# Compression with token pairs stationary over four column groups; queries, scores and top-k in four parts of two heads

## The chip, the cores and the metric

The kernel runs on one core of one Trainium2 chip, in float32 throughout. The metric is the device time of one execution in microseconds (us), the median over the runs shown. TensorE (PE) multiplies matrices, VectorE (DVE), ScalarE (ACT) and GpSimd (POOL) do the elementwise work, SyncE (SP) issues the plain loads and stores, and 16 DMA engines move the data.

## The reference, cut to what matters

One decoder layer on a prompt of 512 tokens and on 8 decoding sequences of 4 tokens (32 rows). After an attention and convolution half comes PEER: every token picks 16 experts for each of 8 heads and adds their rows.

```python
# compress: 16-token chunks; a block's hidden row is the sum over its two chunks
parts = jnp.einsum('bcsgd,jsdh->jbcgh', r, w1c)          # w1: 2048 x 256 for keys and for values
hid = b1 + pe.reshape(-1) @ w1
for j in range(ratio): hid = hid + parts[j, :, j:j + nc]
out = jax.nn.gelu(hid) @ w2 + b2
# peer: D_MODEL 1024, 8 heads, 128 keys a half, 16384 experts
q = (xb @ q_w).reshape(PEER_BLOCK, PEER_HEADS, 2, PEER_DQ // 2)
s = jnp.einsum('thcd,hcnd->thcn', q, sub_keys)
s1, i1 = lax.top_k(s[:, :, 0], PEER_TOPK); s2, i2 = lax.top_k(s[:, :, 1], PEER_TOPK)
cand = s1[..., :, None] + s2[..., None, :]               # 256 candidates, of which top_k takes 16
u = eu[eidx]; v = ev[eidx]                               # rows of 1024 floats each
a = jax.nn.gelu(jnp.einsum('td,thkd->thk', xb, u))
return jnp.einsum('thk,thkd->td', g * a, v)
```

## The kernel before, in words

The tokens are worked on in five tiles: four of 128 prompt rows (0 to 3) and tile 4 with the 32 sample rows. For a tile of 128 rows, PEER needs 128 "rows" of the stream: row n is one head and one rank, and one indirect DMA of POOL (L1950) gathers for it the expert's u and v for all 128 tokens, 1 MB. Tile 4 packs four heads on the partitions and needs 32. So 544 gathers flow through a ring of 10 buffers (`RING`, tile `expert_rows`). For each row DVE makes the dot product with h2 (L1906), ACT makes the gelu, the weight and a diagonal (L1386, L1392, L1402), and PE multiplies diagonal by v into four banks (L1044, L1047 for tile 4). POOL issues the gather of row n when PE has freed row n - 10.

Everything else of a tile (norm, input products, compression, attention, convolution, output product, queries, scores and top-k) is **side work**, written as stages that are cut into slots (generators that `yield`). Tile 0's side work runs ahead of the stream (the first window), and that of tiles 1 to 4 inside it: `slots_before` spreads the slots over the rows in proportion to lengths given in `SLOTS_OF` (in rows), so that the last slot comes at row 500. Before row n each engine runs all slots that `e.before` gives, in the order of the plan (`make_plan`); a list of lists in the plan holds lanes whose slots go in step. PE runs four rows ahead (`LEAD`). PE, ACT and DVE each have one fixed order, so whatever waits in a slot holds back the rows behind it.

The side weights come in units of 1 MB through 3 slots (`SLOTS`, tile `weight_units`), issued by SP in the order of use; the load of unit j waits until unit j - 3 was used. Side work uses four banks in turn (`Products`).

The stages of the change. **cmp(i)** (PE L728, 16 slots of PE's own): 4 units of w1 (keys and values, 2 each), for each 8 positions and 2 halves of the hidden width a product with the 128x128 weights stationary and 14 to 21 chunk columns moving; then gelu (ACT L1188), w2 (PE L745) and the key norm. It is 22 slots and 11 rows long, in a lane with att(i); conv(i), the 124 taps of DVE (L1518), three in a slot, is the other lane. For tile 0 the convolution is POOL's and the other lane is a gap of 22 slots and ada2, which takes 12 units of w_ada (L608). **query0(i)** turns h2 (L882), makes the first 8 query columns from 4 units of peer_q (L848) and their scores with a unit of keys of 512 KB (L870); **query1(i)** does the second half. **topk0(i), topk1(i)** (DVE L1707 to L1758) pick the experts of four heads each; topk0 stands in a lane beside query1, topk1 beside the x and glu stages of the next tile. POOL waits for topk0 before a tile's first row and for topk1 before its row 64.

## Time and profile before

| | us |
|---|---|
| median of 3 runs | 2129.03 |
| lowest, highest | 2128.95, 2151.08 |
| span of the profiled execution, first to last instruction | 2124.2 |

The profiled execution's own time is not listed apart from its span; the lowest run and the median are 4.8 us above that span. In the span PE is busy 1587.9 us (75%), DVE 1232.5 (58%), ACT 781.4 (37%) and POOL 701.2 (33%). The DMA engines move 782.11 MB, of which the gathers' queue has 570.46, at a mean of 368 GB/s. In a table of windows, the DMA column is the busy share of the 16 DMA engines and the last one what they moved.

### The profile page before, as it was taken

What the parts mean: (1) busy time and instruction counts of PE and PEld (TensorE: products, weight loads), DVE (VectorE), ACT (ScalarE), POOL (GpSimd) and SP (SyncE); (2) the same over time, 40 slices, a digit from 0 to 9 for tenths busy, and PEclk for the clock granted to TensorE, in tenths of its full rate; (3) what the DMA queues carried; (4) which work ended last, traced back from release to release, by engine and by line L of the source; (5) the groups of instructions that cost most, each with busy time, mean ns of one, the idle gap of its engine ahead of it and who ended that gap; (6) DMA issues with size and microseconds to landing.
All of it is one profiled execution on the core that took longest, in us unless ns stands there. A gap on an engine that the chain in (4) does not pass through costs nothing.

```text
span 2124.2 us, 29781 instructions
## 1 busy us (share of the span) xinstructions
PE 1587.9 (75%) x10176; PEld 954.1 (45%) x10176; DVE 1232.5 (58%) x3327; ACT 781.4 (37%) x2217; POOL 701.2 (33%) x611
## 2 busy tenths in 40 slices
PE   6976658795967788758888685889687786759533
PEld 4845534443644445535534363556254342426200
DVE  0132566794586795488598459643555353443754
ACT  2132144384245375334367422352412132332322
POOL 0850112342323343223443322434323323323442
PEclk9786878687979699879888887969889868778765
DMA  7773899998999989899999998999989988999996
GB/s 270 244 288 109 328 376 426 422 364 366 375 394 426 421 369 396 353 426 378 424 426 359 393 398 351 426 378 396 425 321 389 384 329 320 375 419 370 417 417 284
DMA packets 149994, 782.11 MB, mean 368 GB/s; under 512 B 17392, under 2 KB 53136, under 8 KB 60932
## 3 DMA queue, kind: packets, MB, share of 16 engines
q0 software_dynamic: 78336, 570.46, 65.1%
q1 hardware_dynamic: 71509, 209.77, 25.9%
q8 instruction: 81, 1.33, 0.2%
q14 instruction: 68, 0.56, 0.1%
HBM read 773.75 MB, written 10.99 MB: 369 GB/s over the span
## 4 chain that ended last, share of the span: by engine, by line
PE 39%; DMA 24%; DVE 18%; issue 8%; ACT 7%; SPq 2%; POOL 1%; POOLq 0%; ACTq 0%; DVEq 0%
DMA expert_rows<-in_expert_uv,expert_index 16%; PE bank L1044 13%; DVE expert_rows L1906 6%; PE bank L921 5%; PE bank L848 5%; PE bank L728 3%; PE bank L667 3%; PE bank L832 3%; DMA gate_or_shift_and_scale<-mod_dram 2%; DVE conv_out L1518 2%; PE bank L639 2%; DMA weight_units<-in_w_ada_units 2%; DMA weight_units<-in_w_out_units 2%; POOL expert_rows L1950 1%; PE bank L999 1%
## 5 line engine op out<-in xcount | busy, mean ns | idle before, releaser
L1950 POOL DMA_INDIRECT expert_rows<-in_expert_uv,expert_index x544 | 629.3, 1157 | 1333.4 <-PE bank L1044 1086.4
L1906 DVE CUSTOM_DVE_ANT_0 expert_rows<-expert_rows,h_rows 128x1024 f32<-128x1024 f32 x544 | 658.8, 1222 | 384.7 <-DMA expert_rows<-in_expert_uv,expert_index 374.1
L1044 PE MATMUL bank<-expert_rows,weight_diagonals 64*64 64x512 f32 x4096 | 605.3, 716 | 104.3 <-ACT weight_diagonals L1402 83.5
L1386 ACT ACTIVATE group_gelu<-group_dots 128x2 f32<-128x2 f32 x272 | 55.5, 204 | 804.4 <-DVE group_dots L1906 790.6
L1044 PEld LDWEIGHTS bank<-expert_rows,weight_diagonals 64*64 64x64 f32 x4096 | 151.4, 153 | 364.8 <-issue 216.8
L848 PEld LDWEIGHTS bank<-stage_room,weight_units 128*128 128x128 f32 x1280 | 153.7, 200 | 37.6 <-issue 31.4
L1402 ACT ACTIVATE weight_diagonals<-consts_sb,group_weights 128x64 f32<-128x64 f32 (+1 forms) x544 | 158.8, 340 | 17.1 <-ACT group_weights L1392 0.7
L848 PE MATMUL bank<-stage_room,weight_units 128*128 128x128 f32 (+1 forms) x1280 | 161.2, 286 | 4.3 <-ACT stage_room L1275 3.5
L1392 ACT ACTIVATE group_weights<-group_gelu,expert_gate 128x1 f32<-128x1 f32 x544 | 131.3, 288 | 9.4
L921 PE MATMUL bank<-weight_units,prompt_bias 128*128 128x256 f32 x512 | 128.7, 401 | 0.0
L1518 DVE SCALAR_TENSOR_TENSOR conv_out<-stage_room,small_weights,conv_out 128x128 f32<-128x128 f32 (+1 forms) x480 | 125.1, 319 | 0.0
L921 PEld LDWEIGHTS bank<-weight_units,prompt_bias 128*128 128x128 f32 x512 | 97.3, 198 | 39.1 <-issue 27.0
L1386 ACT ACT_TABLE_LOAD x81 | 103.9, 1283 | 1.4
L728 PEld LDWEIGHTS bank<-compress_pairs,weight_units 128*128 128x128 f32 x512 | 85.0, 262 | 27.8 <-issue 27.8
L832 PE MATMUL bank<-weight_units,stage_room 128*128 128x256 f32 (+1 forms) x320 | 77.7, 401 | 22.7 <-DVE stage_room L1662 17.8
L667 PE MATMUL bank<-weight_units,stage_room 128*128 128x256 f32 (+1 forms) x400 | 92.6, 387 | 2.6 <-DMA weight_units<-in_w_in_units 2.6
L639 PEld LDWEIGHTS bank<-stage_room,weight_units 128*128 128x128 f32 x640 | 82.0, 211 | 27.7 <-issue 15.9
L639 PE MATMUL bank<-stage_room,weight_units 128*128 128x128 f32 (+1 forms) x640 | 85.5, 297 | 8.9 <-ACT stage_room L1109 8.9
L728 PE MATMUL bank<-compress_pairs,weight_units 128*128 128x16 f32 (+1 forms) x512 | 87.0, 321 | 0.0
L667 PEld LDWEIGHTS bank<-weight_units,stage_room 128*128 128x128 f32 (+1 forms) x400 | 68.8, 176 | 33.4 <-issue 17.0
L832 PEld LDWEIGHTS bank<-weight_units,stage_room 128*128 128x128 f32 (+1 forms) x320 | 57.0, 182 | 47.8 <-DVE stage_room L1662 21.9
L1047 PE MATMUL bank<-expert_rows,weight_diagonals 128*32 128x512 f32 x128 | 28.8, 1052 | 53.7 <-ACT weight_diagonals L1402 43.5
(250 smaller groups left out, 1648.2 us busy)
## 6 DMA issues: line engine op xcount, KB each, us to landing
weight_units<-in_w_in_units SPq DMA_DIRECT2D x45, 1024.0 KB
weight_units<-in_peer_q_units SPq DMA_DIRECT2D x40, 1024.0 KB
weight_units<-in_w_ada_units SPq DMA_DIRECT2D x24, 1024.0 KB
weight_units<-in_w_out_units SPq DMA_DIRECT2D x20, 1024.0 KB
weight_units<-in_w_units SPq DMA_DIRECT2D x16, 1024.0 KB
expert_rows<-in_expert_uv,expert_index POOLq DMA_INDIRECT x544
weight_units<-in_cmp_pages SPq DMA_DIRECT2D x128, 64.0 KB
gate_or_shift_and_scale<-mod_dram SPq DMA_DIRECT2D x12, 512.0 KB
```

Source lines behind the costliest of these rows:

```text
L639: last = mm(out[:, a * P:a * P + r], w[:, k, a * P:(a + 1) * P], hT(i, k), start=(k == 0), stop=(k == KD - 1))
L667: last = mm(out[0:r, c * 256:(c + 1) * 256], hT(i, k), w[:, k], start=(k == 0), stop=(k == KD - 1))
L728: last = mm(out[:, c:c + g3 * n].rearrange("p (g c) -> p g c", g=g3), w[:, s, hh * P:(hh + 1) * P], e.rT[:, kv, s, 0:g3, one + lo:one + hi ...
L832: last = mm(out[0:r, 0:256], e.catT[:, k, 0:r], w[:, k], start=(k == 0), stop=(k == KD - 1))
L848: last = mm(out[:, c:c + r], w[:, k, a * P:(a + 1) * P], e.h2T[:, k, 0:r], start=(k == 0), stop=(k == KD - 1))
L921: last = mm(dst, e.w1_s[:, one, s, hh * P:(hh + 1) * P], w[:, :, :, s], start=False, stop=(one == 1 and s == 7))
L1044: last = mm(e.bank[2 * a + c][o * HD:(o + 1) * HD, :], e.diag[ps, m % (NG * GR)], e.ring[ps, m % RING, cs], start=first, stop=final)
L1386: do(e.act_v[:, p], e.dots[:, p], ACT.Gelu_apprx_tanh).then_inc(e.s_gelu, 1)
L1402: do(e.diag[:, p * GR + j, 0:unit.shape[1]], unit, ACT.Copy, scale=e.wv[:, p, j:j + 1]).then_inc(e.s_d, 1)
L1518: ins = vec.scalar_tensor_tensor(out, src, w[:, ct, k:k + 1], out, ALU.mult, ALU.add)
L1906: vec.tensor_tensor_reduce(out=row, in0=row, in1=e.h2[:, i % 2], scale=1.0, scalar=0.0, op0=ALU.mult, op1=ALU.add, accum_out=e.dots[:, q % ...
L1950: pool.indirect_dma_start(e.ring[:, n % RING], None, e.io["expert_uv"], bass.IndirectOffsetOnAxis(ap=e.eidx[:, i % 2, j:j + 1], axis=0)).t ...
```

## The change

The compression turns its product round: 16 chunks of both groups (32 columns) are stationary, the 256 weight columns move, and four positions go at a time to the four groups of 32 columns of the array; ACT copies the four partial sums from the bank (`e.parts`), and four products with a stack of identities add them and turn them. The chunks lie by chunk and group in `e.rT`, the position encodings in chunk columns 9 and 10 for tile 0. The stage is 11 slots and 5.5 rows long.

Queries, scores and top-k go in four parts. One stage `query` has 37 slots; the scores of part q are made within the next part's query products; the keys come in four units of 256 KB. The four stages topk0 to topk3 take two heads each, 20 slots. For tile 0 only topk0 is in the first window, and topk1 to topk3 stand beside ada3, a pad of 36 slots (9 rows), x and glu of tile 1. For tiles 1 to 3 topk0 and topk1 stand beside the query stage (after a gap of 12 slots), topk2 and topk3 beside x and glu of the next tile. POOL waits for a part before every 32nd row. `slots_before` lets mix(i) for i > 1 begin no sooner than 8 rows into the tile before, and finds the pace by bisection.

```diff
-    e.rT = pairs[:].rearrange("p (a s g c) -> p a s g c", a=2, s=8, g=3)
+    pairs = e.sb("compress_pairs", [P, 1536])
+    e.rT = pairs[:, 0:2 * 8 * CHUNKS * G].rearrange("p (a s c g) -> p a s c g", a=2, s=8, g=G)
...
-    e.scores = [room[:, a:a + 1024].rearrange("p (a n) -> p a n", a=PH) for a in (1024, 3072)]
-    e.top16 = [Top16(room[:, 4096:4864], room[:, 4864:4992]), Top16(room[:, 2304:3072], room[:, 4096:4224])]
+    e.scores = [room[:, a:a + 512].rearrange("p (a n) -> p a n", a=4) for a in (1024, 1536, 3072, 3584)]
+    e.top16 = Top16(room[:, 4096:4416], room[:, 5048:5176])
...
-            "conv": (43, 0), "cmp": (22, 11), "mix": (18, 10), "query0": (20, 11), "query1": (19, 12.5), "topk0": (31, 8),
-            "topk1": (31, 9), "sc": (42, 24), "satt": (90, 44)}
+            "conv": (43, 0), "cmp": (11, 5.5), "mix": (18, 10), "query": (37, 23.5), "topk": (20, 5), "sc": (42, 24), "satt": (90, 44)}
...
+    def chain(i, ahead, behind):
+        return [[ahead + [("x", i), ("glu", i)], behind], ("z", i),
                 [[("cmp", i), ("att", i)], [("conv", i)]],
-                ("mix", i), ("query0", i), [[("query1", i)], [("topk0", i)]]]
+                ("mix", i), [[("query", i)], [("gap", 12), ("topk0", i), ("topk1", i)]]]
+
+    def late(i):
+        return [("topk2", i), ("topk3", i)]
 
     windows = [[("ada1", 0), ("x", 0), ("glu", 0), ("z", 0),
                 [[("cmp", 0), ("att", 0)], [("gap", 22), ("ada2", 0)]],
-                ("mix", 0), ("query0", 0), [[("query1", 0)], [("topk0", 0)]]]]
-    windows.append(chain(1, [("ada3", 0)]))
+                ("mix", 0), [[("query", 0)], [("gap", 12), ("topk0", 0)]]]]
+    windows.append(chain(1, [("ada3", 0), ("pad", 36)], [("topk1", 0)] + late(0)))
     for i in range(2, PT):
-        windows.append(chain(i, []))
-    windows.append([[[("sc", 0), ("x", PT), ("glu", PT)], [("topk1", PT - 1)]], ("sc", 1), ("z", PT),
+        windows.append(chain(i, [], late(i - 1)))
+    windows.append([[[("sc", 0), ("x", PT), ("glu", PT)], late(PT - 1)], ("sc", 1), ("z", PT),
...
+    items = [item for w in windows[1:] for item in w]
+    room, low, high = FIRST[PT] - 12.0, 0.5, 2.0
+    for _ in range(40):
+        pace = (low + high) / 2
+        ends, done, begun = [0.0], {}, {}
+        for item in items:
+            start = ends[-1]
+            for lane in lanes_of(item):
+                at = len(ends) - 1
+                for name, i in lane:
+                    begun[name, i] = at
+                    at += size_of(name, i)[0]
+                    done[name, i] = at
+                    if name == "mix" and i > 1:
+                        start = max(start, FIRST[i - 1] + 8.0)
+            k = slots_of(item)
+            ends += [start + pace * length_of(item) * (s + 1) / k for s in range(k)]
+        low, high = (pace, high) if ends[-1] < room else (low, pace)
...
+def query_units(i):
+
+    out = [("pq", i, u) for u in range(8)]
+    if i == PT:
+        return out + [("keys", i, q) for q in range(4)]
+    for q in range(3):
+        out.insert(3 * q + 3, ("keys", i, q))
+    return out + [("keys", i, 3)]
...
-        out = prod.open(pe, ("hid", i))
         for kv in range(2):
+            out = prod.open(pe, ("part", i, kv))
             for one in range(2):
                 w = units.take(("w1", i, kv, one)).rearrange("p (k n) -> p k n", k=8)
                 for s in range(8):
-                    for hh in range(2):
-                        c = (2 * kv + hh) * g3 * n
-                        last = mm(out[:, c:c + g3 * n].rearrange("p (g c) -> p g c", g=g3), w[:, s, hh * P:(hh + 1) * P],
-                                  e.rT[:, kv, s, 0:g3, one + lo:one + hi],
-                                  start=(kv == one == s == hh == 0), stop=(kv == one == hh == 1 and s == 7))
-                    if s % 2 and s < 7:
-                        yield
-                if kv == 0 or one == 0:
+                    j = 32 * (s % 4)
+                    last = mm(out[j:j + 32, 0:256], e.rT[:, kv, s, lo + one:lo + one + 16].rearrange("p c g -> p (c g)"),
+                              w[:, s], start=(one == 0 and s < 4), stop=(one == 1 and s >= 4))
+                if one == 0:
                     units.used(last)
                     yield
+            last.then_inc(prod.ready, 1)
+            units.used_by(("part", i, kv))
+            yield
+        prod.freed(pe, ("part", i, 1))
+        out = prod.open(pe, ("hid", i))
+        for a in range(4):
+            last = mm(out[:, a * 32:(a + 1) * 32], e.parts[:, a // 2, a % 2 * P:(a % 2 + 1) * P],
+                      e.consts[:, C_STACK:C_STACK + NS], start=True, stop=True)
...
+    def scores_of(i, q, out):
+        keys = key_part(i, q)
+        prod.freed(pe, ("pq", i, q))
+        for a in range(4):
+            last = mm(out[:, a * P:(a + 1) * P], e.q2T[:, 4 * (q % 2) + a, 0:P], keys[:, a], start=True, stop=True)
+        last.then_inc(prod.ready, 1)
+        units.used_by(("scores", i, q))
+
+    def query(i):
         r = rows(i)
-        for u in us:
-            w = units.take(("pq", i, u)).rearrange("p (k n) -> p k n", k=KD)
+        pe.wait_ge(e.s_h2, i + 1)
+        for q in range(2):
+            out = prod.open(pe, ("h2T", i, q))
+            for k in range(4):
+                last = turn(out[:, k * r:(k + 1) * r], e.h2[0:r, i % 2, (4 * q + k) * P:(4 * q + k + 1) * P],
+                            ident[0:r, 0:r])
+            last.then_inc(prod.ready, 1)
+        yield
+        prod.freed(pe, ("h2T", i, 1))
+        for u in range(8):
+            w, j = units.take(("pq", i, u)).rearrange("p (k n) -> p k n", k=KD), units.n - 1
+            q = u // 2
             if u % 2 == 0:
-                out = prod.open(pe, ("pq", i, u // 2))
+                if q and i < PT:
+                    last_scores = prod.open(pe, ("scores", i, q - 1))
+                out = prod.open(pe, ("pq", i, q))
             for a in range(2):
                 c = (u % 2 * 2 + a) * P
                 for k in range(KD):
@@ -851,61 +900,30 @@
                         yield
                 if a == 0:
                     yield
+                    if u % 2 == 0 and q and i < PT:
+                        scores_of(i, q - 1, last_scores)
             if u % 2:
                 last.then_inc(prod.ready, 1)
-                units.used_by(("pq", i, u // 2))
+                units.used_by(("pq", i, q), j)
             else:
+                units.used(last, j)
+            yield
+        yield
+        if i < PT:
+            yield
+            scores_of(i, 3, prod.open(pe, ("scores", i, 3)))
...
+        for kv in range(2):
+            yield
+            if kv:
+                yield
+            out = prod.wait(act, ("part", i, kv))
+            nc.scalar.copy(e.parts[:, kv], out[:, 0:256]).then_inc(prod.free(("part", i, kv)), 1)
...
+        def kept(q):
+            out = prod.wait(act, ("scores", i, q))
+            nc.scalar.copy(e.scores[q].rearrange("p a n -> p (a n)"), out[:]).then_inc(prod.free(("scores", i, q)), 1)
+
+        for q in range(4):
+            for _ in range(3):
+                yield
+            if q and i < PT:
+                kept(q - 1)
+            for _ in range(6 if q == 0 else 5):
                 yield
             out = prod.wait(act, ("pq", i, q))
             dst = e.q2T_s[:, 4 * q:4 * q + 4, 0:r] if i == PT else e.q2T[:, 4 * (q % 2):4 * (q % 2) + 4, 0:r]
             nc.scalar.copy(dst, out[:].rearrange("p (a n) -> p a n", a=4)[:, :, 0:r]
                            ).then_inc(prod.free(("pq", i, q)), 1)
-        if i == PT and half == 0:
-            return
-        for q in range(2 if i < PT else 1):
-            key = ("scores", i, 2 * half + q if i < PT else 0)
-            out = prod.wait(act, key)
-            dst = e.scores[half if i < PT else 0][:, 4 * q:4 * q + 4]
-            nc.scalar.copy(dst.rearrange("p a n -> p (a n)"), out[:]).then_inc(prod.free(key), 1)
-            if q == 0:
-                yield
+        for _ in range(3):
+            yield
+        kept(3 if i < PT else 0)
...
-        for a in range(nh // 2):
-            prod.freed(dve, ("scores", i, 2 * part + a))
-            yield from top16(scores, keep.half, keep.half_i, range(4 * a, 4 * a + 4))
+        prod.freed(dve, ("scores", i, part))
+        yield from top16(scores, keep.half, keep.half_i, range(4))
         pair = keep.half[:, 0:2 * nh].rearrange("p (h c) k -> p h c k", c=2)
         link(vec.tensor_tensor(grid, span(pair[:, :, 0], 3, TK), span(pair[:, :, 1], 2, TK), ALU.add))
         yield
-        for a in range(nh // 2):
-            yield from top16(cand, keep.top, keep.top_i, range(2 * a, 2 * a + 2))
+        yield from top16(cand, keep.top, keep.top_i, range(2))
...
-            if j % 64 == 0:
-                pool.wait_ge(e.s_rt, 2 * i + j // 64 + 1)
+            if j % 32 == 0:
+                pool.wait_ge(e.s_rt, 4 * i + j // 32 + 1)
...
-            sp.dma_start(slot[:, 0:D], io["keys_unit"][:, key[2] * D:(key[2] + 1) * D]).then_inc(sem, 16)
+            sp.dma_start(slot[:, 0:4 * P], io["keys_unit"][:, key[2] * 4 * P:(key[2] + 1) * 4 * P]).then_inc(sem, 16)
```

## Rows read from the trace of the kernel before

**Rows 1.** Windows, columns as in the header; before the stream, the stream, its end.
```profile
core 0: us, PE busy (x) PEld busy (x) DVE busy (x) ACT busy (x) POOL busy (x), PEclk, DMA share, GB/s
0.00:254.70 254.70, 191.99 (x1335) 156.85 (x1335) 75.28 (x292) 63.41 (x169) 71.90 (x67) 0.84 0.67 241
...
255.00:2108.00 1853.00, 1392.26 (x8825) 796.67 (x8825) 1149.59 (x3025) 715.72 (x2041) 629.02 (x544) 0.82 0.95 389
2030.00:2100.00 70.00, 23.38 (x104) 3.56 (x96) 38.12 (x60) 18.57 (x72) 27.74 (x24) 0.57 1.01 419
```

**Rows 2.** POOL in order of time: the first gather, with its wait.
```profile
254.74 1.14 POOL L1950 DMA_INDIRECT expert_rows<-in_expert_uv,expert_index  x1 [119.70 <-DVE expert_index L1752]
```

**Rows 3.** PE in order of time: tile 0's compression, units of w_ada, first queries.
```profile
83.64 27.34 PE L728 MATMUL bank<-compress_pairs,weight_units 128*128 128x21 f32 x128
...
121.08 3.36 PE L608 MATMUL bank<-weight_units,y_half_sums 128*32 128x256 f32 x32
...
142.32 1.07 PE L608 MATMUL bank<-weight_units,y_half_sums 128*32 128x256 f32 x16
...
206.40 15.95 PE L848 MATMUL bank<-stage_room,weight_units 128*128 128x128 f32 x128 [0.68 <-ACT stage_room L1275]
```

**Rows 4.** ACT in order of time: the copy of the first query bank.
```profile
215.24 0.59 ACT L1287 COPY stage_room<-bank 128x512 f32<-128x512 f32 x1 [8.89 <-PE bank L848]
```

**Rows 5.** DVE in order of time: the first readers of compression and of attention scores.
```profile
111.02 0.16 DVE L1570 TENSOR_TENSOR hidden_bias<-bank,small_weights 128x4 f32<-128x4 f32 x1 [27.70 <-PE bank L728]
...
121.30 0.29 DVE L1612 CUSTOM_DVE_ANT_0 stage_room<-bank,prompt_bias 128x128 f32<-128x128 f32 x1 [2.35 <-PE bank L771]
```

**Rows 6.** The chain that ended last, 224 to 254 us: topk0 of tile 0.
```profile
224.86 0.88 DVE stage_room L1707 x4
...
230.06 0.89 DVE stage_room L1707 x4
...
235.27 1.24 DVE stage_room L1730
236.51 0.02 issue
...
240.74 0.76 DVE stage_room L1707 x2
...
244.94 0.22 DVE expert_gate L1735
...
245.81 1.23 DVE stage_room L1744
...
253.61 0.20 DVE expert_index L1752
```

**Rows 7.** Windows: the first tile's attention, its query stage, the first rows.
```profile
84.00:121.00 37.00, 30.39 (x150) 29.93 (x149) 3.33 (x8) 5.23 (x10) 34.65 (x31) 0.50 0.55 187
121.00:152.00 31.00, 24.51 (x258) 12.84 (x259) 11.56 (x53) 10.25 (x42) 13.12 (x12) 0.95 0.91 353
...
206.40:254.70 48.30, 39.51 (x356) 35.73 (x356) 28.88 (x115) 8.80 (x15) 0.00 (x0) 0.96 0.76 271
...
280.00:300.00 20.00, 10.43 (x68) 6.53 (x72) 17.14 (x66) 10.92 (x29) 1.93 (x2) 0.63 0.76 295
```

**Rows 8.** Windows in the stream: compression of tiles 2, 3; attention of 1, 2.
```profile
700.00:740.00 40.00, 32.57 (x223) 19.97 (x222) 24.70 (x70) 12.03 (x36) 14.69 (x14) 0.76 1.01 418
1020.00:1075.00 55.00, 47.09 (x317) 26.14 (x309) 39.82 (x100) 17.30 (x64) 24.92 (x21) 0.78 1.01 424
421.00:480.00 59.00, 51.74 (x328) 27.58 (x332) 55.43 (x195) 49.15 (x134) 26.08 (x20) 0.86 0.93 368
750.00:810.00 60.00, 53.91 (x361) 28.89 (x361) 58.00 (x198) 53.12 (x141) 29.13 (x22) 0.97 0.99 411
```

**Rows 9.** Windows of line L1518 alone (convolution taps), columns DVE, PEclk, DMA.
```profile
421.00:480.00 59.00, 16.04 (x56) 0.86 0.93 368
```

**Rows 10.** The chain that ended last: the landing of a lone w_out unit.
```profile
499.96 9.98 DMA weight_units<-in_w_out_units
```

**Rows 11.** Tile weight_units, 480 to 640 us: tile 1's query products.
```profile
L848 PE MATMUL bank<-stage_room,weight_units x256: 274/275/579, 530.7 to 580.0; 128*128 128x128 f32 x128
```

**Rows 12.** Line L848: what its engine waited for, in the whole span.
```profile
  DMA weight_units<-in_peer_q_units: 1.7, 3
```

**Rows 13.** The page: DMA issues, size of a unit of peer_q.
```profile
weight_units<-in_peer_q_units SPq DMA_DIRECT2D x40, 1024.0 KB
```

More of the change, by code:

```diff
@@ L403, in size_of @@
         return i, 0
+    if name == "pad":
+        return i, i / 4
+    if name.startswith("topk"):
+        return SLOTS_OF["topk"]
     if name == "att":
@@ L517, in weight_units @@
         "mix": lambda i: [("wo", i, q) for q in range(4)],
-        "query0": lambda i: [("pq", i, u) for u in range(4)] + ([("keys", i, 0)] if i < PT else []),
-        "query1": lambda i: [("pq", i, u) for u in range(4, 8)] + ([("keys", i, 0)] if i == PT else []) + [("keys", i, 1)],
+        "query": query_units,
         "sc": lambda part: [("pages", part // 2, part % 2 * 2 + s) for s in range(2)],
@@ new lines, in query @@
+        yield
+        if i < PT:
+            yield
+            scores_of(i, 3, prod.open(pe, ("scores", i, 3)))
+            return
+        prod.freed(pe, ("pq", i, 3))
+        out = prod.open(pe, ("scores", i, 0))
+        for q in range(4):
+            keys = key_part(i, q)
+            for a in range(4):
+                last = mm(out[q * NS:(q + 1) * NS, a * P:(a + 1) * P], e.q2T_s[:, 4 * q + a, 0:NS], keys[:, a],
+                          start=True, stop=True)
+            if q < 3:
+                units.used(last)
@@ L910, in sc @@
+        last.then_inc(prod.ready, 1)
+        units.used_by(("scores", i, 0))
     def sc(part):
@@ L1565, in cmp @@
         b2 = e.col("b2").rearrange("p (a d) -> p a d", a=2)
-        for _ in range(15):
+        for _ in range(4):
             yield
```

188 lines of the change are left out of this document (63 added, 125 removed).

## The prediction

> **What bounds the kernel now.** I read the windows of long stretches first. They cut the execution in two. Up to the first gather at 254.7 us the DMA engines are busy 67% of the time, at 241 GB/s; from there to 2108 us they are busy 95%, at 389 GB/s; and at the end, where no side work is left, gathers alone move 419 GB/s [rows 1]. PE, DVE and ACT are far from full in the stream as a whole (1392, 1150 and 716 of 1853 us). So the stream is close to a transfer bound, with 5% idle, 93 us, and the time before it is a chain of latencies in which a third, 84 us, is DMA idle. The timeline of POOL shows what ends that chain: POOL had been waiting 119.7 us for the expert index when the first gather went out at 254.74 [rows 2]. Every microsecond taken from that chain starts the stream earlier. It is worth a microsecond at the end only if the DMA engines were idle in it, because the bytes are the same.
>
> **The sum is made against the span, 2124.2 us.** The median 2129.0 is 4.8 above it, and I carry that 4.8 over.
>
> **Compression of tile 0.** PE works on it from 83.64 for 27.3 us, at the lower clock (0.50, 1.2 GHz), in 128 records for 64 products of 21 columns [rows 3, 7]; its first reader gets it at 111.02 [rows 5]. The new form has 32 products, 64 records, of the form of the w_ada products (32 columns stationary, 256 moving, four column groups). There 32 records took 3.36 us at 121.08, just out of the low clock, and 16 took 1.07 at 142.32 [rows 3]. So 4.3 to 6.7 us; I take 6.7 for the clock. Only 3 units fit ahead, and the fourth is asked for after the first was used, at 85.3. A unit is 1 MB [rows 13], 2.5 us at 419 GB/s, so it lands about 88 and holds nobody up by more than a microsecond. New are two copies by ACT and four products with identities: the copies take half of a 0.59 us copy of 512 columns [rows 4] each, the eight records under 0.4 us each, so 3 us on the path. 83.6 + 6.7 + 3.1 = 93.4 against 111.0: **17.6 us** earlier. The bounds are 12 (the fourth unit late by 5) and 20 (full clock).
>
> **Attention of tile 0.** It shares its slots with ada2, whose 12 MB took the 31 us from 121 to 152 at a DMA share of 0.91 [rows 7]. ada2 now begins 11 attention slots later and leaves 5 after it instead of 16, so what comes earlier at one side comes back at the other: 0, between -4 and +4. Attention starts at 121.30 [rows 5] and takes longer than those 31 us, so even 17.6 us earlier it ends after POOL's convolution, which is done by 254.74 - 119.70 = 135.0 [rows 2].
>
> **Query and top-k of tile 0.** Queries begin at 206.40, DVE's first top-k instruction runs at 224.86 [rows 3, 6], so 18.5 us. Now the first bank is ready after two units (its copy starts 8.8 us in [rows 4]), the scores follow half a unit later (2 us), with 1.1 us of products and 0.6 of copy: 12.5, **6.0 us** less. Top-k of four heads ran from 224.86 to 253.81. Four lists of 128 cost 5.2 (224.86 to 230.06), the candidates 1.24, two lists of 256 4.2 (236.53 to 240.74), and the rest 8.9, of which 7.4 are six instructions of 1.24 over all candidates [rows 6]. For two heads that is 5.2 + 0.65 + 4.2 + 5.3 = 15.3 against 28.9: **13.6 us** less. The first gather comes 17.6 + 6.0 + 13.6 = 37 us earlier.
>
> **What is paid back.** The 17.6 us of compression lie in a stretch with a DMA share of 0.55 [rows 7]; its loads fit into what is left of it, so that part is kept. The 19.6 of query and top-k don't: from 206.40 to 254.70 the DMA moved 48.3 x 271 = 13.1 MB [rows 7]. By the new first gather only 4.75 units of it, 5.0 MB, will have been asked for; the last query units, two units of keys, ada3 and what tile 1 asks for, 8.1 MB, now run beside the gathers. At 419 GB/s that is 19 us of a full resource. From 280 to 300 us the share was 0.76 [rows 7], 5 us of idle that the extra loads can use in part, the more so as a pad of 9 rows moves tile 1's loads away from the first rows. I take 16, between 0 (if rows are paced by something else than DMA) and 20.
>
> **Compression in the stream.** For tiles 1 to 3 PE is relieved of some 20 us each. But in tile 2's and tile 3's compression the DMA share is 1.01 [rows 8] with PE 81 and 86% busy: the rows didn't wait for PE. Its 4 MB now come within 8 to 10 rows instead of 18, and the rows freed are handed to other stages, since the plan still ends at row 500. 0, at best -15, if the relieved PE shortens the stalls at the changes of stage.
>
> **Convolution beside attention.** DVE's 43 slots of taps now lie over 11 slots of compression and 30 of attention instead of 22 and 21: 27 taps more in attention. In tile 1's attention DVE is 55.4 of 59 us busy and the DMA share falls to 0.93; in tile 2's it is 58.0 of 60 [rows 8]. The taps there cost 16.04 us for 56 [rows 9], so 27 are 7.7 us a tile, on an engine that is full. The ring of 10 hides some of it, and tile 3 has three rows more for its attention. I take 5 for all three, between 0 and 23.
>
> **Look-ahead of the weights.** Keys in four units put a small unit between the peer_q units, and of the 3 slots one then holds 256 KB. The load of peer_q units 3 to 7 is asked for one unit's time ahead instead of two. A unit's time in tile 1 is (580.0 - 530.7) / 8 = 6.2 us [rows 11]; a lone unit took 9.98 to land under gathers [rows 10]. The wait by this is 3.8 us for every second unit, 1.9 on average, 5 units in 3 tiles: 28 us of PE. Against it, PE waited 1.7 us in all for peer_q units before [rows 12], and PE's waits are covered by rows in flight as long as the DMA queue is full, as it is there. I take 5, between 0 and 28.
>
> The Trainium skill says, in "DMA: Bandwidth & Descriptors", Queues, rings and completion order, that each engine goes round between the queues it has work for, packet by packet. By that rule, a lone unit beside the gathers would get half of the engines, about 5 us, the look-ahead term would be 0 and the time 2113. The measured 9.98 us speaks against equal halves.
>
> **Top-k and small things.** Twice as many parts cost DVE 16 x 15.3 against 8 x 28.9, 14 us over 500 rows, in stages where DMA is the limit, and ACT eight exponentials more with their table loads: 0, at most +5. After row 500 nothing changes.
>
> **The sum:** 2129.0 - 37 + 16 + 5 + 5 = 2118 us.
>
> **The rivals.**
> - **Nothing is paid back.** Rows are paced by DVE, ACT and PE after all, extra loads slip into the 5% of idle, or the relieved PE gives as much as is paid. For: 93 us of idle are there, and the rate of 389 is below 419. Against: it sits in short stalls, not in the first rows. 2129 - 37 = 2092, down to 2077 with the relief. Chance 0.28.
> - **The loads of peer_q come too late** (the slower side). In the query stage PE waits for units 3 to 7 and the rows queue behind it. It decides once a load lands later than one unit's time, 6.2 us. Full price 28 us: 2118 - 5 + 28 = 2141, slower by 12; above 1% if loads take 13 us. Chance 0.12.
> - **DVE bound in attention** at full price: 2118 - 5 + 23 = 2136. Chance 0.08.
> - **The start doesn't move by the compression**, since ada2's 12 MB begin later and set the end of attention: 2118 + 17 = 2135. Chance 0.04.
>
> **How the numbers follow.** My forecast, 2118 with a range of its own of 2103 to 2132, has 0.48. A difference of 1%, 21 us, is about what a measurement can tell from none. Faster by more: the first rival and the lower edge of the forecast, 0.28 + 0.07 = 0.35. Slower by more: the far end of the look-ahead case, 0.07. The rest, 0.58, within 1%. The range reaches from 2085, inside the first rival, to 2142, and leaves out the relief on top of a full gain and loads of 13 us, about 0.2.
>
> **What would show it.** The first gather at about 217 us; compression's first reader near 93; topk0 15 us long; the DMA share full from the first gather to row 40 and row 40 reached some 20 us earlier, not 37; DVE over 97% in tile 1's attention; PE's waits for peer_q units above 1.7 us. I'd be wrong if row 40 came 35 us earlier (first rival), or if windows of the query stages grew (second).

## The result, and the profile after

The changed kernel takes **2157.7 us** in the median (2142.5 to 2162.7, 4 runs), the kernel before 2134.8 in the same rounds: a ratio of **1.010 [1.006, 1.015]**, slower by 1%, where 2118 (2085 to 2142) was forecast. A later run of the change with one gap moved (e3) gave 1.011. The profiled execution took 2142.5 us, the fastest of the four; its span is 2140.7 against 2124.2. The waits that are quoted below for e2 and e3 come from executions 1.5% and more above the fastest of their kernels, so only large differences in them count.

The page, busy time by engine, and windows in the columns of [rows 1]: before the stream, the stream, its end.
```profile
PE 1550.3 (72%) x9952; PEld 901.7 (42%) x9952; DVE 1253.6 (59%) x3463; ACT 796.9 (37%) x2244; POOL 691.8 (32%) x611
```
```profile
0.00:224.40 224.40, 162.79 (x1135) 124.97 (x1136) 68.05 (x245) 59.35 (x163) 72.02 (x67) 0.85 0.66 238
225.00:2124.00 1899.00, 1383.23 (x8798) 775.56 (x8796) 1177.63 (x3207) 735.32 (x2074) 619.20 (x544) 0.82 0.95 384
2047.00:2117.00 70.00, 22.20 (x104) 3.77 (x104) 38.24 (x61) 19.04 (x74) 28.93 (x24) 0.60 1.01 415
```
The start did get shorter, by 30 us; the stream is 46 us longer, at the same DMA share of 0.95 and 384 instead of 389 GB/s. So DMA engines are as "busy" as before and move less in a microsecond; a share of busy time doesn't show that. Time times rate gives the bytes: 61.4 MB came before the first gather, now 53.4, and the missing 8.0 MB have to come in the stream. At 389 GB/s they take 21 of the 46 us, an estimate. The other 25 are the lower rate.

POOL in order of time: the first gather, which answers to [rows 2].
```profile
224.44 1.14 POOL L1965 DMA_INDIRECT expert_rows<-in_expert_uv,expert_index  x1 [89.81 <-DVE expert_index L1767]
```
It is 30.3 us earlier, not 37. The chain that ended last shows the compression, DVE the first readers [rows 5].
```profile
83.33 1.91 PE bank L750 x16
85.26 8.24 DMA weight_units<-in_w_units
93.55 1.98 PE bank L750 x16
95.55 0.38 ACT stage_room L1203
95.97 1.93 PE bank L761 x8
```
```profile
97.93 0.16 DVE L1589 TENSOR_TENSOR hidden_bias<-bank,small_weights 128x4 f32<-128x4 f32 x1 [15.12 <-PE bank L761]
...
108.50 0.29 DVE L1631 CUSTOM_DVE_ANT_0 stage_room<-bank,prompt_bias 128x128 f32<-128x128 f32 x1 [2.36 <-PE bank L797]
```
The products are short, but the fourth unit of weights took 8.24 us from its request to its landing. No gather runs yet, but SP asks for the rows of the adaptation's bias, the prompt's bias (2 MB by the last line, which is from the list of DMA issues: KB, and us to landing) and the first w_ada unit (1 MB) right behind it:
```profile
86.75 0.39 SPq L2097 DMA_DIRECT2D prompt_bias<-in_bias_prompt  x1
87.19 0.30 SPq L2098 DMA_DIRECT2D page_ids<-in_page_table  x1
87.54 0.89 SPq L1982 DMA_DIRECT2D weight_units<-in_w_ada_units  x1
...
prompt_bias<-in_bias_prompt SPq DMA_DIRECT2D x1, 2048.0 KB, 11.6
```
The reader is 13.1 us earlier than in [rows 5]. Then the queries on PE, and DVE's first and last instruction of topk0:
```profile
195.50 10.81 PE L897 MATMUL bank<-stage_room,weight_units 128*128 128x128 f32 x80 [0.68 <-ACT stage_room L1298]
```
```profile
207.86 0.88 DVE L1724 MAX8 stage_room<-stage_room 128x8 f32<-128x128 f32 x4 [15.06 <-ACT stage_room L1303]
...
223.31 0.18 DVE L1767 CAST expert_index<-stage_room 128x32 int32<-128x32 f32 x1
```
Queries begin 10.9 us earlier [rows 3], so attention, with ada2 in it, gave back 2.2; topk0 starts 12.4 us after them instead of 18.5, and is over in 15.6 us instead of 28.9 [rows 6].

**In the stream** I counted DVE's expert products in order of time (one for each row of experts) in both traces. Difference to before, us, for the change and for some of the runs below:
```
row            0     8    40    64   128   208   304   400   504   543
change     -23.1 -22.5 -15.0  -7.5  +4.5  +5.6  +6.2 +12.3 +16.8 +16.7
e1         -13.1 -14.9 -12.8 -13.4 -15.3 -22.3 -24.9 -17.3 -11.3 -10.2
e7         -39.1 -17.9 -14.9 -15.5 -20.4  -6.0 -14.9  +8.8  +9.4 +12.9
e13        -32.4 -18.3 -15.0 -16.4  -9.1 -19.5 -33.4 -16.5 -13.0 -14.3
e17        -26.3  -5.9  -9.5  +0.3  -3.8  +4.1  -7.5 +11.5 +10.5  +9.0
```
Of 30.3 us half is given back by row 40, as forecast. The other half and 4 us more go between rows 40 and 128, and 12 more by the end. Executions of one kernel differ by up to 35 us, so only the large steps count.

The windows from the first gather to row 8, to row 40 and to row 128, before and after, tell what was paid with bytes:
```profile
254.74:308.33 53.59, 20.62 (x140) 12.97 (x141) 28.43 (x110) 17.20 (x39) 14.57 (x16) 0.63 0.91 372
308.33:421.12 112.79, 93.65 (x581) 56.52 (x579) 74.80 (x188) 43.07 (x118) 35.75 (x33) 0.80 1.01 424
421.12:723.59 302.47, 241.48 (x1574) 150.66 (x1574) 216.54 (x635) 143.04 (x387) 99.99 (x84) 0.84 0.95 389
```
```profile
224.44:285.80 61.36, 31.38 (x206) 15.38 (x208) 28.44 (x103) 12.30 (x31) 15.92 (x16) 0.68 0.98 400
285.80:406.11 120.31, 84.50 (x595) 48.44 (x591) 79.71 (x226) 55.14 (x137) 33.66 (x30) 0.81 0.95 388
406.11:728.08 321.97, 246.14 (x1602) 147.46 (x1598) 228.79 (x705) 149.91 (x402) 102.65 (x90) 0.82 0.96 386
```
Up to row 8 there are 4.6 MB more, and 7.8 us. From row 8 to 40 there is 1 MB less, and still 7.5 us more: the rate fell from 424 to 388 GB/s. From row 40 to 128 there are 6.6 MB more, and 19.5 us.

PE in order of time, tile 1's query stage: products with peer_q units (L897); under it SP's requests, where x2 are two requests in a row.
```profile
551.90 1.06 PE L897 MATMUL bank<-stage_room,weight_units 128*128 128x128 f32 x8
554.76 1.16 PE L897 MATMUL bank<-stage_room,weight_units 128*128 128x128 f32 x8
559.53 4.43 PE L897 MATMUL bank<-stage_room,weight_units 128*128 128x128 f32 x24 [3.61 <-DMA weight_units<-in_peer_q_units]
...
576.00 3.84 PE L897 MATMUL bank<-stage_room,weight_units 128*128 128x128 f32 x32 [2.37 <-DMA weight_units<-in_peer_q_units]
584.70 3.63 PE L897 MATMUL bank<-stage_room,weight_units 128*128 128x128 f32 x16 [2.98 <-DMA weight_units<-in_peer_q_units]
```
```profile
543.77 0.33 SPq L1992 DMA_DIRECT2D weight_units<-in_keys_unit  x1
549.41 6.87 SPq L1990 DMA_DIRECT2D weight_units<-in_peer_q_units  x2
```
Keys take one of the three weight slots at 543.8, the next peer_q unit can only be asked for at 549.4, and PE gets it at 559.5, 10.1 us later: the 9.98 of [rows 10] again. The waits of the whole span (us in total, times, longest) are 28.5 us of PE, 25.8 of them in tiles 1 to 3. Before, PE itself had 0.6; the 1.7 of [rows 12] holds the waits of its weight loads too, and counted so the change has 62.0. The second line is DVE's wait for scores, which was 26.0 in 3 waits before.
```profile
PE bank L897 <- DMA weight_units<-in_peer_q_units: 28.5, 14, 3.7
DVE stage_room L1724 <- ACT stage_room L1303: 64.3, 5, 15.6
DVE expert_rows L1921 <- DMA expert_rows<-in_expert_uv,expert_index: 286.9, 178, 10.7
```
The third line was 374.1 us before. So DVE now waits less for the rows' own data, while POOL waits longer until PE frees a buffer, 1140.7 us against 1086.4. How long tile 1's eight units take on PE shows in the first and last start of their products, in the change and in e4 below, which gives peer_q all three weight slots:
```profile
L897 PE MATMUL bank<-stage_room,weight_units x256: 274/275/583, 535.7 to 596.4; 128*128 128x128 f32 x128
```
```profile
L896 PE MATMUL bank<-stage_room,weight_units x256: 275/275/579, 542.3 to 591.5; 128*128 128x128 f32 x128
```
That is 60.7 and 49.2 us, where [rows 11] have 49.3.

Windows of the query stages of tiles 1 to 3, before and after. In each of the six PE multiplies 24 rows (192 records of L1044 or L1062).
```profile
528.00:610.00 82.00, 65.35 (x488) 43.72 (x488) 56.31 (x164) 24.26 (x73) 26.41 (x24) 0.87 0.95 393
865.00:946.00 81.00, 63.64 (x484) 41.12 (x482) 54.27 (x158) 22.62 (x73) 24.83 (x24) 0.88 0.92 381
1227.00:1304.00 77.00, 62.67 (x486) 41.41 (x484) 54.88 (x160) 22.84 (x73) 25.72 (x24) 0.92 0.98 404
```
```profile
533.00:622.00 89.00, 66.02 (x490) 46.44 (x491) 61.05 (x190) 30.61 (x82) 28.08 (x24) 0.86 0.90 358
866.00:952.00 86.00, 63.60 (x489) 44.06 (x488) 59.97 (x190) 29.40 (x81) 24.42 (x24) 0.90 0.90 364
1234.00:1319.00 85.00, 67.77 (x488) 47.51 (x488) 58.11 (x177) 24.64 (x73) 24.04 (x23) 0.86 0.90 351
```
The same rows and the same work take 5 to 8 us more, 20 in all, and the bytes in them are the same too, 94 MB before and 93 after: what fell is the rate. The DMA share was 0.92 to 0.98 before and is 0.90 in all three, at 351 to 364 GB/s. Here the transfer queue does run short, and 20 of the 25 us of lower rate lie here.

Attention of tiles 1 to 3 after the change, and the convolution taps alone in it, which answers to [rows 8, 9]:
```profile
412.00:483.00 71.00, 58.77 (x332) 30.76 (x332) 63.76 (x226) 47.86 (x132) 24.15 (x22) 0.78 0.98 399
739.00:815.00 76.00, 62.66 (x418) 33.16 (x418) 73.88 (x238) 52.97 (x147) 33.46 (x25) 0.92 0.94 393
1073.00:1166.00 93.00, 79.46 (x518) 42.95 (x514) 79.32 (x246) 60.82 (x164) 37.97 (x33) 0.93 0.97 380
```
```profile
412.00:483.00 71.00, 24.77 (x87) 0.78 0.98 399
```
31 tap instructions more cost 8.7 us there. DVE is 90% busy in tile 1's attention, not over 97, and 97% in tile 2's.

### The profile page after: what moved, and what is told of

Same layout as the page of the kernel before. It is cut to its first block, busy times and chain, and to the rows that moved or that the text cites. A ratio compares the mean times of both kernels' runs of the same rounds, so it can differ in the third digit from the quotient of the medians.

```text
span 2140.7 us, 29552 instructions
## 1 busy us (share of the span) xinstructions
PE 1550.3 (72%) x9952; PEld 901.7 (42%) x9952; DVE 1253.6 (59%) x3463; ACT 796.9 (37%) x2244; POOL 691.8 (32%) x611
## 4 chain that ended last, share of the span: by engine, by line
PE 41%; DMA 23%; DVE 17%; issue 8%; ACT 7%; SPq 4%; POOL 1%; another core or an unknown queue 0%; POOLq 0%; ACTq 0%; DVEq 0%
PE bank L1062 12%; DMA expert_rows<-in_expert_uv,expert_index 8%; DVE expert_rows L1921 6%; PE bank L939 6%; PE bank L897 5%; DMA weight_units<-in_peer_q_units 4%; PE bank L858 3%; PE bank L692 3%; PE bank L664 3%; DVE conv_out L1537 2%; DMA gate_or_shift_and_scale<-mod_dram 2%; DMA weight_units<-in_w_ada_units 2%; DMA weight_units<-in_w_units 2%; SPq L2003 2%; SPq L2008 1%
## 5 line engine op out<-in xcount | busy, mean ns | idle before, releaser
L1965 POOL DMA_INDIRECT expert_rows<-in_expert_uv,expert_index x544 | 619.8, 1139 | 1359.1 <-PE bank L1062 1140.7
L1062 PE MATMUL bank<-expert_rows,weight_diagonals 64*64 64x512 f32 x4096 | 594.7, 707 | 122.9 <-ACT weight_diagonals L1421 100.0
L1062 PEld LDWEIGHTS bank<-expert_rows,weight_diagonals 64*64 64x64 f32 x4096 | 152.4, 153 | 398.0 <-issue 228.8
L897 PE MATMUL bank<-stage_room,weight_units 128*128 128x128 f32 (+1 forms) x1280 | 175.9, 299 | 31.8 <-DMA weight_units<-in_peer_q_units 28.5
L897 PEld LDWEIGHTS bank<-stage_room,weight_units 128*128 128x128 f32 x1280 | 166.2, 212 | 64.4 <-DMA weight_units<-in_peer_q_units 33.5
L664 PE MATMUL bank<-stage_room,weight_units 128*128 128x128 f32 (+1 forms) x640 | 86.9, 299 | 14.1 <-ACT stage_room L1127 9.6
L664 PEld LDWEIGHTS bank<-stage_room,weight_units 128*128 128x128 f32 x640 | 83.4, 214 | 31.5 <-issue 20.4
L1065 PE MATMUL bank<-expert_rows,weight_diagonals 128*32 128x512 f32 x128 | 28.7, 1046 | 54.9 <-ACT weight_diagonals L1421 44.0
L1724 DVE MAX8 stage_room<-stage_room 128x8 f32<-128x128 f32 (+1 forms) x102 | 27.6, 326 | 64.7 <-ACT stage_room L1303 64.3
L797 PE MATMUL bank<-prompt_keys_values,queries_turned 64*128 64x128 f32 (+3 forms) x128 | 55.5, 544 | 10.6 <-ACT compressed_keys L1220 6.4
```

Source lines behind the costliest of these rows:

```text
L664: last = mm(out[:, a * P:a * P + r], w[:, k, a * P:(a + 1) * P], hT(i, k), start=(k == 0), stop=(k == KD - 1))
L897: last = mm(out[:, c:c + r], w[:, k, a * P:(a + 1) * P], e.h2T[:, k, 0:r], start=(k == 0), stop=(k == KD - 1))
L1062: last = mm(e.bank[2 * a + c][o * HD:(o + 1) * HD, :], e.diag[ps, m % (NG * GR)], e.ring[ps, m % RING, cs], start=first, stop=final)
L1965: pool.indirect_dma_start(e.ring[:, n % RING], None, e.io["expert_uv"], bass.IndirectOffsetOnAxis(ap=e.eidx[:, i % 2, j:j + 1], axis=0)).t ...
```

## The experiments

Ratios are to the kernel before, in 5 rounds, with the 95% interval. 1% is 21 us. "Weight slots" are the three for weight units; slots without that word are steps of the plan. "+-" is the 95% uncertainty of a difference, worked out from the two intervals. The edits are cut to the lines that matter, and a comment says what else goes with them.

**e1, the new compression alone**, in before, over 11 rows as there.
```
-"cmp": (22, 11)
+"cmp": (11, 11)      # and cmp of PE, ACT, DVE, e.rT, e.parts as in the change
```


> The kernel before with the new compression alone, in 11 slots; its planned length stays 11 rows. Theory A (the loss of the change comes from query and top-k in four parts: DVE waits for the first scores in the stream, and PE for peer_q units; compression's gain at the start is kept): 10 to 17 us faster than before, ratio 0.992 to 0.995, first gather 12 to 17 us earlier. Rival B (DVE bound in attention, since the taps are spread over it, eats the gain): same as before or up to 10 us slower, rows of the attention of tiles 1 to 3 take 5 to 8 us longer each.


**0.9907 [0.9873, 0.9942]**, 2114.6 us. Faster, by 12 to 27 us; the first gather is 13.0 us earlier (241.73), so the start alone could be all of it. In the profiled execution the lead grows to 25 us in the stream and shrinks at the end. In the chain, the fourth unit of its weights again:
```profile
83.59 7.13 DMA weight_units<-in_w_units
```

**e2, the four parts alone**: the changed kernel with the old compression.
```
-"cmp": (11, 5.5)     # and cmp, e.rT as before
+"cmp": (22, 11)
```


> The changed kernel with the compression of before (128 columns stationary, 22 slots, 11 rows). Theory A: the losses are all here, the gain of compression is missing: 25 to 45 us slower than before, ratio 1.012 to 1.02. Rival B: nearly no loss in the stream, 0 to 10 us slower or faster.


**1.0072 [1.0035, 1.0109]**, with 28.7 us of waits for peer_q. So the loss belongs to the parts, though alone they lose less than the 1.2 to 2% expected. The two halves multiply to 0.998 and together give 1.010, 1.2 +- 0.7% more: they also disturb each other.

**e3, top-k later.**
```
-[("gap", 12), ("topk0", i), ("topk1", i)]
+[("gap", 20), ("topk0", i), ("topk1", i)]
```


> The changed kernel with a gap of 20 slots instead of 12 ahead of topk0 in the stream. DVE waited 12.8, 14.8 and 15.6 us for the first scores of tiles 1 to 3. Theory A1 (that wait holds the dot products back and with them the ring): the waits shrink to under 4 us each and the time falls by 8 to 20 us against the change, ratio to before 1.001 to 1.006. Rival A2 (rows in flight cover it): the waits go and the time stays, ratio 1.008 to 1.012.


**1.0113 [1.0060, 1.0167]**. DVE's waits for scores halve (the 15.2 left in one piece is tile 0's, ahead of the stream), and nothing is won:
```profile
DVE stage_room L1724 <- ACT stage_room L1303: 31.9, 5, 15.2
PE bank L897 <- DMA weight_units<-in_peer_q_units: 25.5, 13, 4.3
```

**e4, the keys elsewhere**: tiles 0 to 3 load them into 512 free columns of the stage room, and peer_q has all three weight slots.
```
+e.keys_r = room[:, 4416:4928]            # loaded once the scores before are made; with its load and its waits
-        out.insert(3 * q + 3, ("keys", i, q))
```


> The changed kernel with the keys of tiles 0 to 3 loaded to a place of their own (columns of stage_room that are free in this stage) instead of through the three weight slots, so peer_q units are asked for two units' time ahead as before. Theory A2 (look-ahead): PE's waits for peer_q fall from 28.5 to under 5 us and the time by 8 to 20 us, ratio to before 1.001 to 1.006; first gather some 5 us earlier, at 219. Rival A1: waits go, time stays within 4 us of the change.


**1.0015 [0.9987, 1.0043]**, 0.9 +- 0.5% less than the change. The first gather came at 226.69, 2.3 us later than the change's, not at 219. PE no longer has such a wait in the list, its weight loads have
```profile
PEld bank L896 <- DMA weight_units<-in_peer_q_units: 3.7, 5, 1.0
```
The eight units' time is back at that of before (49.2 us, above), and so are the query stages. These are their windows in e4, 24 rows of PE each; the columns are PE and PEld for the rows' products alone:
```profile
539.00:621.00 82.00, 26.58 (x192) 6.81 (x192) 0.85 0.93 384
865.00:948.00 83.00, 26.86 (x192) 6.73 (x192) 0.87 0.92 383
1231.00:1311.00 80.00, 28.57 (x192) 7.02 (x192) 0.84 0.98 400
```
They take 245 us, where before has 240 and the change 260, and the DMA share is 0.92 to 0.98 again. The late loads are the largest single item.

**e5, compression planned over 11 rows** in the changed kernel.
```
-"cmp": (11, 5.5)
+"cmp": (11, 11)
```


> The changed kernel with one number changed: the compression stage keeps its 11 slots but is planned 11 rows long instead of 5.5, so attention and convolution of tiles 1 to 3 get more rows. The kernel with the new compression alone, planned so, was 0.9907 of before, the change 1.0102, and the change with the old compression 1.0072. Theory D (density: in the change attention with its taps is packed into 22 rows where DVE is full, and this eats what the compression gives): 10 to 20 us faster than the change, ratio to before 0.998 to 1.003. Rival (the parts spoil the gain whatever the plan): ratio 1.008 to 1.012.


**1.0056 [1.0025, 1.0087]**: 0.5% less, with intervals that overlap, and between the two forecasts.

**e6, the stream packed as in the change**, but in e1.
```
-"cmp": (11, 11)
+"cmp": (11, 5.5)     # glu of tiles 1 to 3: (18, 15.5) instead of (18, 10)
```


> The kernel before with the new compression alone, but planned as in the change: the compression 5.5 rows long, and glu of tiles 1 to 3 5.5 rows longer, so that everything after attention keeps its rows. Only attention and taps are packed. Theory D: 8 to 20 us slower than with 11 rows (0.9907), ratio 0.995 to 1.000, rows 40 to 64 take 5 to 10 us longer. Rival: 0.989 to 0.993.


**0.9924 [0.9894, 0.9954]**, 0.2% above e1 and not told apart from it. The taps beside attention cost little by themselves.

**e7 and e8, e4 with compression over 11 rows**, and that with the gap of 20.
```
+"cmp": (11, 11)
+("gap", 20)          # e8 alone
```


> The change with the keys in a place of their own (1.0015 alone) and the compression planned 11 rows long. If look-ahead and density are separate losses they add: ratio 0.990 to 0.996, peer_q waits under 5 us. If they are one (both only shift where the rows wait): 0.999 to 1.002.

> The same with a gap of 20 slots ahead of topk0 in the stream. By the theory that DVE's waits for scores cost once the weights are not late: 3 to 10 us faster than without. By the rival (rows in flight cover them): within 3 us of it.


**1.0005 [0.9974, 1.0037]** and **0.9977 [0.9952, 1.0003]**. From e4 to e7 it is 0.1 +- 0.4%, from e7 to e8 0.3 +- 0.4%. The 0.5% of e5 isn't seen here, so nothing shows that it is a price of its own. 0.7 +- 0.4% to e1 is still open.

**e9, e1 with the pad**: tile 1's x and glu begin 9 rows later, and all that follows is planned closer.
```
-windows.append(chain(1, [("ada3", 0)]))
+windows.append(chain(1, [("ada3", 0), ("pad", 36)]))   # and the pad's length, a quarter row a slot
```


> The kernel before with the new compression alone (0.9907 of before), and on top of it the changed kernel's pad of 36 slots (9 rows) ahead of tile 1, so that every later stage is planned closer together. If the pad and the denser plan behind it are what the parts still lose once their look-ahead is restored (0.7%, 15 us), this is 0.997. If they cost nothing, 0.990.


**0.9956 [0.9927, 0.9985]**, 0.5 +- 0.5% above e1.

**e10, e8 without the exponentials of the top-k.**
```
-do(g, g, ACT.Exp)
+do(g, g, ACT.Copy)                       # the semaphore that follows it stays
```


> The changed kernel with keys outside of the weight slots, compression over 11 rows and a gap of 20 (0.9977 of before), with the 17 exponentials of the top-k replaced by copies: the softmax is left out, the waits and the order stay. If twice as many exponentials, with their table loads between the rows' gelus, are the 15 us that are left, this is 0.991 or less; a kernel with nine would gain half as much. If ACT's side is covered, 0.997.


**0.9979 [0.9949, 1.0009]**, as e8. ACT's groups of instructions in e8 and, in the second fence, here: besides the 17 table loads of the exponentials (21.8 us) 12 table loads of the rows' gelus go.
```profile
L1404 ACT ACT_TABLE_LOAD x83 | 106.5, 1283 | 2.0 <-DVE group_dots L1921 0.5
L1325 ACT ACT_TABLE_LOAD x17 | 21.8, 1283 | 0.3
```
```profile
L1404 ACT ACT_TABLE_LOAD x71 | 91.1, 1283 | 1.6 <-DVE group_dots L1921 0.4
```
37 us of ACT are worth 0.0 +- 0.4%: to within 8 us its side is covered.

**e11, e8 with half of the top-k left out; e12, the same in e1.**
```
+if i < PT and part >= 2:                 # e12: part >= 1
+    ...                                   # gs and eidx of this part are copied from part 0
+    return
```


> The same kernel (0.9977), with the top-k of the third and fourth part of tiles 0 to 3 left out: they take the first part's indices and weights, at the same slots. Some 12 us of DVE work go from each stretch in which the next tile's x and glu begin. If late top-k on DVE, ahead of glu's first step, is the 15 us, this gains at least that: 0.990 or less, and more than the next run gains on its own base. If DVE is covered there, 0.997.

> The control: the kernel before with the new compression alone (0.9907), with the second top-k of tiles 0 to 3 left out, which lies beside the next tile's x and glu: it takes the first one's indices and weights. The same work goes from DVE as in the run before. If DVE limits the rows there in the two-part form as well, 0.985 or less; if late top-k costs only in four parts, 0.990.


**0.9927 [0.9893, 0.9961]**, 0.5 +- 0.4% below e8, and **0.9898 [0.9863, 0.9933]**, 0.1 +- 0.5% below e1. The same DVE work may be dearer in the four-part form, but the difference, 0.4 +- 0.7%, doesn't show it.

**e13, a shorter pad** in e8, and **e15, in the changed kernel**. Some pad there must be: ACT's x of tile 1 waits for topk1 of tile 0, which has 20 slots.
```
-("pad", 36)
+("pad", 16)
```


> The changed kernel with keys outside of the weight slots, compression over 11 rows and a gap of 20 (0.9977 of before), its pad cut from 36 slots to 16. The pad cost 0.5% on top of the new compression alone; if it costs the same here, 20 of its 36 slots are worth 0.3%: 0.995. If the pad only cost there because no top-k in four parts lies beside it (without it the four parts would have to be waited for anyway), this stays 0.998.

> The changed kernel (1.0102, 1.0113 with a gap of 20) with nothing but the pad cut from 36 slots to 16. 1.007 if the pad's price adds to the others; 1.010 if the late loads of peer_q set the rows there anyway.


**0.9955 [0.9926, 0.9984]**, 0.2 +- 0.4% below e8, and **1.0148 [1.0097, 1.0198]**, above the change and above both forecasts, with 33.7 us of waits for peer_q. The pad's 0.5% of e9 is not confirmed inside the four parts.

**e14, e13 with the third top-k part later; e16, e1 with its second.**
```
-windows.append(chain(i, [], late(i - 1)))
+windows.append(chain(i, [], [("gap", 8)] + late(i - 1)))   # e16: the same gap ahead of topk1
```


> The same, and a gap of 8 slots ahead of the third top-k part of tiles 1 and 2, so that DVE makes the next tile's x before it starts on top-k, with 48 slots for the same 13 rows. If the late top-k costs its 0.5% because PE's glu waits behind it for DVE's x, 0.002 to 0.004 less than the run before: 0.992. If it costs by the amount of DVE work among the rows, no less, or more: 0.995 or above.

> The kernel before with the new compression alone (0.9907) and a gap of 8 slots ahead of the second top-k of each tile, as a try for a faster kernel: 0.988 if DVE's x and glu steps behind the top-k hold PE up there as well, 0.991 if not (leaving out the second top-k gave 0.9898), more if 39 slots in 13 rows are too close.


**0.9983 [0.9949, 1.0017]** and **0.9955 [0.9926, 0.9985]**, 0.3 and 0.5% worse, each +- 0.5. So nothing is won by letting glu's step go ahead of the top-k; if anything, more slots in the same 13 rows cost.

**e17, e2 with the keys elsewhere.**
```
 "cmp": (22, 11)      # e4's edit
```


> The four-part queries and top-k on the old compression (1.0072 of before), with the keys outside of the weight slots. If the look-ahead of the peer_q loads costs its 0.9% without the new compression too, 0.998. If it costs mainly where the new compression has made the stages denser, 1.003 to 1.007: then the two parts of the change disturb each other there, and the missing sum (0.9907 times 1.0072 is 0.998, the change 1.010) is in it.


**1.0031 [0.9999, 1.0063]**: 0.4% less than e2, where the same edit took 0.9% from the change. The lost look-ahead may cost half as much under the old compression, and part of the disturbance between the two halves may lie here; the two differences (0.4 and 0.9, each good to about 0.5) don't show it.

## Why the prediction was wrong

Its steps in order, with what the traces and runs have in their place.

- **What bounds the kernel.** Right that bytes and a short transfer queue set the stream; but the remark that PE's waits are covered "as long as the DMA queue is full, as it is there" was wrong of the query stages (below).
- **Compression of tile 0, 17.6 us.** Measured 13.1 at the first reader (111.02 to 97.93) and 12.8 at attention's first (121.30 to 108.50). The step "so it lands about 88" failed: 2.5 us is a unit's time at full rate, not the time until it has landed, which was 8.24. The 12 at the lower end named this. So the start came 30.3 us earlier, not 37.
- **Attention, 0.** Minus 2.2, within -4 to 4.
- **Query and top-k, 6.0 and 13.6.** 6.1 and 13.3. Right, by the durations of single instructions.
- **Paid back, 16 us.** The number by row 40, 15, agrees in part by luck. The bytes were worked out rightly: 8.1 MB forecast, 8.0 measured. But by row 40 only 3.5 of them had come, and 7.5 of the 15 us were lost between rows 8 and 40 to a lower rate, for which no run shows a cause. The rest of the bytes came between rows 40 and 128. By an estimate all 8.0 cost 21 us at the stream's own 389 GB/s; the forecast took them at 419 and then from 19 down to 16. That loads which the start skipped are paid for in the stream is seen in e17 too: its first gather is 18.8 us earlier (235.96) and row 8 only 5.9, and the stretch between them moves 26.4 MB against 19.9. In e1, which skips none (61.5 MB before the first gather), nothing of the 13 us is returned by row 40.
- **Compression in the stream, 0, at best -15.** No error shown: e1 is 20 us faster, 12 to 27, and 13 are from the start. In the profiled executions the time from first gather to last row is 1855.8 us against 1853.1.
- **Convolution beside attention, 5 us of 23.** Taps cost 8.7 us of DVE in tile 1, as estimated (7.7). e6 puts what this and the packing cost together at 0.2 +- 0.5%, 4 us, and can't tell it from none. No error shown.
- **Look-ahead of the weights, 5 us of 28: the step that failed.** The waits came as worked out: 25.8 us of PE in tiles 1 to 3 against 28. (The 1.7 set beside them was PE and its weight loads together; PE alone had 0.6.) The size taken for them didn't: removing them (e4) is worth 0.9 +- 0.5%, some 18 us, two thirds of the waits. The step said that rows in flight cover PE's waits as long as the DMA queue is full, "as it is there". It was nearly full there before, 0.92 to 0.98; with the waits it is 0.90, the three query stages take 20 us more for the same 24 rows and the same bytes, and e4 gives 15 of them back and the share too.
- **Top-k and small things, 0 to 5 us.** Perhaps too low. By e11 against e12, late top-k would cost 0.4 +- 0.7% more in four parts than in two, and e14 speaks against one explanation, its place. The pad, which the forecast gave a gain ("moves tile 1's loads away from the first rows"), had no price in the sum: 0.5 +- 0.5% in e9, 0.2 +- 0.4% between e8 and e13.
- **The rule weighed** (the Trainium skill, "DMA: Bandwidth & Descriptors", Queues, rings and completion order: each engine goes round between its queues, packet by packet). The forecast read it as two equal shares, by which a lone unit lands in 5 us and the look-ahead is free. The landings were 9.98 us in [rows 10] and 10.1 at 549.4, but neither unit was alone: two more peer_q units were asked for within the first, one within the second. The queue of plain loads (packets, MB, share of the 16 engines' time) in these two stretches:
```profile
q1 hardware_dynamic: 236, 1.80, 43.0%
```
```profile
q1 hardware_dynamic: 195, 1.44, 36.1%
```
So that queue had less than half, and the unit shared it with those behind it. The look-ahead wasn't free.

In the sum 2129 - 37 + 16 + 5 + 5, the start and what is paid back became -30 + 21, and the 5 for look-ahead about 18. That makes 2143, 1.007 of before; against the measured 1.010 (1.006 to 1.015) some 8 us are not placed, with an interval that reaches down to none. **The rival** "the loads of peer_q come too late" had the mechanism and 2141, and a chance of 0.12; it deserved more, since its condition (a load later than 6.2 us) was met by the only row at hand, 9.98 us.

**What the parts could win at all.** The forecast counted 19.6 us of earlier start for query and top-k, and most of it back. Counted in bytes, e8 moves 54.4 MB before its first gather at 221.84 and e1 61.5 before its own at 241.73. The start is 19.9 us earlier and 7.1 MB are owed, an estimate of 18 us at 389 GB/s. So even with the loads of peer_q mended the four parts had some 2 us to win, and any loss of rate makes them slower than e1.

**What stays open.** e8 has the change's keys, density and scores mended and is still 0.7% above e1; the best four-part form, e13, is 0.5% above e1. Pad and late top-k may each explain a part, within the error of the runs. And why the compression is worth 0.9% in before and 0.2 +- 0.4% in e17's company (1.0031 to e4's 1.0015) wasn't found. The likeliest reading, argued and not shown: the stream has one stretch of slack after another, and the four parts' 30 us earlier start asks for side work in the same rows at a higher pace.

**The version to keep is e1**, 0.9907 of before and 0.981 of the change (0.9907 / 1.0102): the new compression, queries and top-k left as they were.

## What to carry over

When a small item is put in a ring of equal slots, work out when the next large load is asked for, and compare its landing time with the consumer's time for one item; if it lands later, the wait is real. Ask for the cover in the very stage where the wait falls, not in the mean of the stream. An earlier start of a transfer-bound stream pays only if the loads in front of it are done as before: count the bytes that move behind the first gather and divide them by the stream's own rate. Here 13 us of start with no bytes owed were kept (e1), and of 18.8 us with loads owed 13 were gone by row 8 (e17). And test two joined edits apart: here the one was worth 20 us (e1), and the other cost 15 alone (e2) and 42 on top of it (1.0102 against 0.9907).

## What the runs showed of the hardware

A 1 MB unit whose bytes are 2.5 us at 419 GB/s took 8.24 us to land (7.13 in e1) with no gather running. Behind it on the same queue 2 MB of the prompt's bias were asked for 1.5 us later and another unit 2.3 us later, and in the 8.24 us that queue moved 1.90 MB. Which of the loads behind it delayed it wasn't tried. In the same stretch the DMA engines were busy 0.88 of the time and moved 233 GB/s, where gathers alone had 1.01 and 415 to 419: the busy share says little about the rate.

Beside gathers a unit took 10.1 us, while the queue of plain loads had 36% of the engines' time.

And 37 us of ACT, 29 loads of its tables among them, cost nothing that could be measured (e10, +- 8 us), although ACT stands between DVE's product and PE's of every row.
